# A streaming encoder layer on one core: pairs of heads and three score buffers in the second attention, single-row events, dense tiles routed earlier

## The chip, the cores and the metric

The kernel runs on one core of a Trainium2 chip. A core has a matrix engine (PE, TensorE), a vector engine (DVE, VectorE), a scalar engine (ACT, ScalarE), a general engine (POOL, GpSimd), a queue engine (SP, SyncE) and 16 DMA engines between the chip's memory and the core's own memories, SBUF and PSUM. The metric is the device time of one execution in microseconds (us), as the median of three runs.

## The reference

One layer runs over 1024 prompt frames and 32 new frames of a running stream, all in float32:

```python
proj = x @ w_in                                   # q, k, v, latents, gates
o_a = stick_breaking_attend(sb_q, k_sb, v_sb)     # first attention, 8 heads of 64
s = (q_nope @ k_nope.T + q_pe @ k_pe.T) * (64 + 32) ** -0.5
p = softmax(where(mask, s, NEG_INF))              # second attention ("MLA"), 8 heads of 64
o_b = p @ v_mla
m = (sigmoid(g_a) * (o_a @ w_oa) + sigmoid(g_b) * (o_b @ w_ob)) @ w_out
h = layer_norm(ALPHA * x + m)
# PEER: per frame and head the 16 best of 128 x 128 experts, by two lists of 128 keys
s1, i1 = top_k(q1 @ keys1.T, 16); s2, i2 = top_k(q2 @ keys2.T, 16)
top_s, pos = top_k(s1[:, None] + s2[None, :], 16)
ff = sum(softmax(top_s) * gelu(u[expert] . h) * v[expert])
y = layer_norm(ALPHA * h + ff)
```

In the second attention a frame reads all keys up to the end of its own chunk of 64 frames. The experts are 16384 pairs of rows (u, v) of 1024 elements each.

## The kernel before

Frames are cut into tiles of 128 (0 to 7) and the sample tile of 32 new frames. They are worked through in three groups, (0, 1, sample), (2, 3, 4) and (5, 6, 7), called groups 0, 1 and 2 here. Each group runs six blocks in a row: `project`, `stick_attend`, `mla_project`, `mla_attend`, `merge_norm`, `score_experts`. After the last group one more block, `dense_experts`, closes the kernel. Between two blocks stands a barrier of all engines: no engine starts the next block before every engine's own sequencer has got through its instructions of the last.

**Two ways to the experts.** For tiles 1, 2 and 3 (the dense tiles) all 16384 experts are computed as matrix products in `dense_experts`, with a table of gates in memory, `gates_by_expert`, that is zero but for the chosen experts. For the other tiles each expert row pair is gathered. One such step, a "row", is one of 16 choices of one head for 128 frames: an indirect DMA from the POOL queue (`fetch`, line 428, 1 MB into one of 9 places of a ring), a dot product on DVE (line 571), gelu and gate on ACT (528, 534), and a weighted addition on DVE four rows later (583). There are 672 rows.

**Routing** is the choice of the experts for one tile and head, a "route": 13 stages of small DVE operations (`route_stage`, `stage`, lines 640 to 670), a softmax after stage 6 and a copy of the indices after stage 12 on ACT. There are 72 routes, in the order of `self.routes`. A route of a dense tile is followed by 16 scatters: indirect DMAs of POOL that add one gate per frame into `gates_by_expert` (`scatter`, line 451). The first scatter of a head waits until all scatters of the same tile's head before have landed.

**What sets the order.** Rows and routes run as background work in the blocks of groups 1 and 2 and in the last block. `SHARES` lists for each block how many rows it takes, how many rows make one event (`batch`), how many heads are routed, and how many scatters it should take. `lay_out` spreads rows and stages evenly into one list of events per block, and `lay_out_loads` places the POOL engine's loads and scatters among them. The foreground code calls `bg.dve(part)` and `bg.act(part)` after each of its steps, which issue the events up to that share; ACT is one step behind DVE. POOL has nothing but this background work in groups 1 and 2, in the order of the events. A row's place of the ring is free when the row five steps earlier has been added.

**The second attention** (`mla_attend`) takes 24 items in each group, one per tile and head. Per item: PE computes scores into one of two score buffers (line 1287); DVE writes the mask, takes the row maximum, and scales it to the exponential's bias (1365, 1368, 1370); ACT takes the exponential with its sum (1335); PE transposes the probabilities by 128x128 (1298) into one PSUM area of 1024 columns; ACT copies them to SBUF in one operation (1346); PE multiplies them with the values, 64 columns per matmul (1309). After the eight heads of a tile DVE multiplies by the inverse sums (1380), PE transposes the result (1321) and DVE copies it to `mla_outT` (1388), which `merge_norm` reads (1506).

## Time and profile before

| | us |
|---|---|
| three runs | 3553.0, 3553.65, 3565.41 |
| median | 3553.65 |
| the profiled execution | 3558.26 |
| its span, first to last instruction | 3556.5 |

| engine | busy us | share of the span |
|---|---|---|
| PE, matmuls | 3036.3 | 85% |
| DVE | 2536.0 | 71% |
| POOL | 1558.1 | 44% |
| ACT | 1210.2 | 34% |

The blocks begin at about these times of the span (PE's first instruction in them):

| | project | stick | mla_project | mla | merge | scores |
|---|---|---|---|---|---|---|
| group 0 | 0 | 154 | 184 | 231 | 275 | 360 |
| group 1 | 436 | 643 | 777 | 827 | 948 | 1054 |
| group 2 | 1161 | 1384 | 1581 | 1638 | 1812 | 1935 |

The last block runs from 2041 to the end. The shares over the whole span are averages over blocks with different limits, so the rows further down are taken block by block. A group of instructions ends with its busy time, the mean of one, and the idle time before it with what ended it; in these, "issue" means that the profile shows nothing that the engine waited for.

### The profile page before, as it was taken

To read this page: it belongs to the slowest core of one execution; us is meant where nothing else is said; L and a number is where in the kernel's file an instruction comes from. 1 tells how busy PE (TensorE), PEld (TensorE's weight loads), DVE (VectorE), ACT (ScalarE), POOL (GpSimd) and SP (SyncE) were. 2 spreads that over 40 slices of the span, in tenths; PEclk is the share of its full clock that TensorE was granted. 3 is DMA by queue.
4 is the path that set the end of the run, shared out by engine and by line. 5 is a ranking of instruction groups with operands and counts; after the bars stand their busy time and mean duration, and the time that the engine had idled before them with its cause. 6 is when DMAs were issued, how large, how long until landed. Compare 5 with 4: busy or idle time off the path is not lost. (4 is left out here: it accounts for less than half of the span.)

```text
span 3556.5 us, 36144 instructions
## 1 busy us (share of the span) xinstructions
PE 3036.3 (85%) x10170; PEld 1717.7 (48%) x10170; DVE 2536.0 (71%) x5041; ACT 1210.2 (34%) x3181; POOL 1558.1 (44%) x1184
## 2 busy tenths in 40 slices
PE   8979989676889895775887898999989999989988
PEld 5755745344545453433654554444444444444443
DVE  0122069887786877877867678888888888788886
ACT  0241234665533435754552322222222222222221
POOL 0000025667662288888777533333333333333330
PEclk9989999785789997997688999999999999999999
DMA  4675589666799997576678999999999999999995
GB/s 144 217 254 177 190 311 394 207 181 202 222 321 359 338 341 218 145 202 181 183 248 301 406 404 399 399 405 396 404 378 412 400 407 398 397 393 407 400 408 204
DMA packets 375912, 1098.51 MB, mean 309 GB/s; under 512 B 91712, under 2 KB 210208, under 8 KB 289568
## 3 DMA queue, kind: packets, MB, share of 16 engines
q0 software_dynamic: 165072, 751.05, 56.6%
q1 hardware_dynamic: 176800, 303.85, 24.4%
q10 hardware_dynamic: 33840, 41.30, 3.3%
q8 instruction: 82, 1.34, 0.2%
q14 instruction: 118, 0.97, 0.1%
HBM read 1031.97 MB, written 63.02 MB: 308 GB/s over the span
## 5 line engine op out<-in xcount | busy, mean ns | idle before, releaser
L428 POOL DMA_INDIRECT expert_rows<-in_experts,picked_index x640 | 770.9, 1204 | 1271.1 <-DVE ff_sum L583 1157.1
L571 DVE SCALAR_TENSOR_TENSOR expert_rows<-expert_rows,h_tile 128x1024 f32<-128x1024 f32 x672 | 820.1, 1220 | 256.8 <-DMA expert_rows<-in_experts,picked_index 212.4
L583 DVE SCALAR_TENSOR_TENSOR ff_sum<-expert_rows,coefficients,ff_sum 128x1024 f32<-128x1024 f32 x672 | 860.8, 1281 | 92.2 <-ACT coefficients L534 75.9
L1786 PE MATMUL dense_act_ps<-dense_hT,key_columns 128*128 128x384 f32 x2048 | 724.7, 510 | 139.5 <-DMA key_columns<-in_key_columns 128.5
L451 POOL DMA_INDIRECT gates_by_expert<-dense_gate,gate_address x384 | 680.3, 1772 | 154.7 <-issue 129.2
L1775 PE MATMUL dense_out_ps<-dense_value_rows,dense_weights 128*128 128x512 f32 x1536 | 678.9, 592 | 0.5 <-DVE dense_weights L1854 0.5
L1786 PEld LDWEIGHTS dense_act_ps<-dense_hT,key_columns 128*128 128x128 f32 x2048 | 399.4, 198 | 482.8 <-DMA key_columns<-in_key_columns 196.2
L833 PE MATMUL proj_ps<-xT,w_in_block 128*128 128x384 f32 (+1 forms) x1392 | 424.1, 468 | 40.7 <-PEq L1595 16.5
L1775 PEld LDWEIGHTS dense_out_ps<-dense_value_rows,dense_weights 128*128 128x128 f32 x1536 | 291.8, 190 | 342.6 <-issue 309.7
L833 PEld LDWEIGHTS proj_ps<-xT,w_in_block 128*128 128x128 f32 x1392 | 268.3, 193 | 195.7 <-issue 37.9
L528 ACT ACTIVATE activated<-dots 128x1 f32<-128x1 f32 (+1 forms) x631 | 124.8, 198 | 638.5 <-DVE expert_rows L571 601.5
L1820 ACT ACTIVATE dense_weights<-dense_act_ps 128x384 f32<-128x384 f32 x128 | 62.5, 488 | 626.0 <-PE dense_act_ps L1786 614.5
L1651 PE MATMUL peer_q_ps<-hT,wq_half 128*128 128x384 f32 (+1 forms) x768 | 239.0, 471 | 16.0 <-PEq L1409 8.2
L375 ACT ACT_TABLE_LOAD x111 | 142.4, 1283 | 269.0 <-DVE top_scores L656 96.5
L1651 PEld LDWEIGHTS peer_q_ps<-hT,wq_half 128*128 128x128 f32 x768 | 148.5, 196 | 97.6 <-issue 15.1
L534 ACT ACTIVATE coefficients<-activated,expert_gate 128x1 f32<-128x1 f32 x640 | 184.1, 294 | 19.7 <-ACT activated L528 0.4
L1287 PE MATMUL score_ps<-mla_kT,mla_qT 96*128 96x512 f32 (+4 forms) x208 | 114.6, 674 | 48.6 <-PEq L1062 48.6
L404 POOL DMA_DIRECT2D expert_scores<-peer_scores x72 | 62.9, 874 | 202.3 <-POOLq L1595 202.2
L1513 PE MATMUL out_ps<-w_out,mergedT 128*128 128x512 f32 (+1 forms) x288 | 130.7, 604 | 3.4 <-DVE mergedT L1568 3.4
L1298 PE MATMUL probsT_ps<-identity,probs 128*128 128x128 f32 (+2 forms) x312 | 66.9, 360 | 67.5 <-ACT probsT L1346 51.6
L528 ACT ACT_TABLE_LOAD x88 | 112.9, 1283 | 27.1 <-DVE expert_rows L571 23.5
L1039 DVE SCALAR_TENSOR_TENSOR softplus<-log_weight_ps,abs_exp_ln 128x512 f32<-128x512 f32 (+2 forms) x78 | 50.8, 651 | 97.1 <-ACT abs_exp_ln L1015 96.5
(186 smaller groups left out, 3144.8 us busy)
## 6 DMA issues: line engine op xcount, KB each, us to landing
key_columns<-in_key_columns SPq DMA_DIRECT2D x128, 512.0 KB, 11.6
dense_value_rows<-in_experts SPq DMA_DIRECT2D x128, 512.0 KB
gates_by_expert<-zeros POOLq DMA_DIRECT2D x12, 2048.0 KB, 21.9
wq_half<-in_peer_wq SPq DMA_DIRECT2D x48, 512.0 KB
dense_gates<-gates_by_expert SPq DMA_DIRECT2D x128, 192.0 KB
w_in_block<-in_w_in ACTq DMA_DIRECT2D x18, 1024.0 KB
w_in_block<-in_w_in SPq DMA_DIRECT2D x18, 1024.0 KB
w_out<-in_w_out SPq DMA_DIRECT2D x24, 512.0 KB, 7.5
```

The source lines that it names most:

```text
L375: act.preload_act_table_set(EXP_LN)
L428: pool.indirect_dma_start(to, None, self.a["experts"], bass.IndirectOffsetOnAxis(ap=index[:, k:k + 1], axis=0)).then_inc(self.got[p % self ...
L451: pool.indirect_dma_start(self.a["gates_by_expert"], bass.IndirectOffsetOnAxis(ap=self.flat[i][:, k:k + 1], axis=0), self.dgate[i][:, k:k ...
L528: act.activation(self.gel[:, k:k + m], self.dots[:, k:k + m], ACT.Gelu).then_inc(self.gelud, m)
L534: act.activation(self.coef[:, c:c + 1], self.gel[:, c:c + 1], ACT.Identity, scale=gate[:, c:c + 1]).then_inc(self.weighed, 1)
L571: dve.scalar_tensor_tensor(place, place, 1.0, self.h[n % 2][:], ALU.mult, ALU.mult, accum_out=self.dots[:, s % TOPK:s % TOPK + 1]).then_in ...
L583: dve.scalar_tensor_tensor(total, self.ring[:, p % self.RING, D:2 * D], self.coef[:, y % TOPK:y % TOPK + 1], total, ALU.mult, ALU.add).the ...
L833: mm = nc.tensor.matmul(out[:, 0:W], w[b % 2][:, k, col:col + P], xT[:, k, :], start=(k == 0), stop=(k == KC - 1))
L1513: mm = nc.tensor.matmul(ps[2 * n + c][0:r, :], f["mergedT"][:, k, at:at + r], w_out[:, k, 512 * c:512 * (c + 1)], start=(k == 0), stop=(k ...
L1651: mm = nc.tensor.matmul(qp[2 * (h % 2) + c][:, 0:W], wq[h % 4][k // 4][:, k % 4, PKEYS * c:PKEYS * (c + 1)], f["hT"][:, k, :], start=(k == ...
L1775: mm = nc.tensor.matmul(out[d][:, 512 * half:512 * (half + 1)], w[e % AB][:, P * d:P * (d + 1)], vals[e % VB][:, 512 * half:512 * (half + ...
L1786: mm = nc.tensor.matmul(up[it % 2][:, 0:W], keys[it % KB][:, k, :], hTd[:, k, :], start=(k == 0), stop=(k == KC - 1))
```

## The change

The change touches four things.

**The second attention.** There are three score buffers of 1024 columns and the scores run two items ahead of the transposes. The transposes go into one bank of 512 columns, so an item with more than four key tiles takes two parts, each copied by ACT before the next is written; ACT's copies keep three buffers `probsT`. The product with the values is made for two heads at a time with the values as the stationary side: it gives the transposed output straight away, 64 rows for each head of the pair. ACT copies it to `mla_outT` once per tile. The scale is folded into `norm_gains` with a minus sign, so that DVE takes a minimum of negated scores and the bias needs no operation of its own. The division by the sums moves to the start of `merge_norm`: three transposes of the inverse sums, a copy on ACT, eight small matmuls that spread them over 64 rows each, and four DVE multiplications of 128x384.

**Rows.** Each row is an event of its own, and ACT collects them (`pending`) until it has `batch` of them, which is 2 in `stick` and `mla`.

**Routes of group 1's tiles.** `self.routes` takes tiles 2 and 3 in pairs two heads after tile 4's first two, so the dense tiles' heads come earlier in the list.

**Scatters.** The last column of `SHARES` for group 2 changes.

```diff
@@ SHARES @@
-        ((2, "project"), 40, 1, 9, 44), ((2, "stick"), 26, 2, 6, 72), ((2, "mla_project"), 7, 1, 2, 26), ((2, "mla"), 25, 2, 5, 70),
-        ((2, "merge"), 20, 1, 2, 48), ((2, "scores"), 29, 1, 0, 40),
+        ((2, "project"), 40, 1, 9, 62), ((2, "stick"), 26, 2, 6, 76), ((2, "mla_project"), 7, 1, 2, 26), ((2, "mla"), 25, 2, 5, 76),
+        ((2, "merge"), 20, 1, 2, 30), ((2, "scores"), 29, 1, 0, 40),
@@ lay_out @@
-        self.routes = [*ahead(0, 1), *heads(SAMPLE), *ahead(4, 2, 3), *heads(5), *heads(6), *heads(7)]
+        pairs = [[(t, h) for t in (2, 3)] for h in range(HEADS)]
+        mixed = [(4, 0), (4, 1), *pairs[0], *pairs[1], (4, 2), *pairs[2], *pairs[3], (4, 3), *pairs[4], *pairs[5], (4, 4), (4, 5), *pairs[6],
+                 (4, 6), *pairs[7], (4, 7)]
+        self.routes = [*ahead(0, 1), *heads(SAMPLE), *mixed, *heads(5), *heads(6), *heads(7)]
...
-                m = min(batch, end - row)
-                due = self.routed_before(row + m - 1) if row < end else 0
+                due = self.routed_before(row) if row < end else 0
...
-                    self.beside[block].append(("rows", row, m))
-                    row += m
+                    self.beside[block].append(("row", row))
+                    row += 1
@@ act @@
-            if e[0] == "rows":
-                self.act_rows(self.nc.scalar, range(e[1], e[1] + e[2]))
+            if e[0] == "row":
+                self.pending.append(e[1])
+                if len(self.pending) == self.batch:
+                    self.act_pending()
...
@@ mla_project @@
+            nc.vector.tensor_scalar(gain[:, 0:QC], gain[:, 0:QC], -MLA_SCALE, None, ALU.mult).then_inc(gain_scaled, 1)
@@ mla_attend, PE @@
+            scores(0)
+            scores(1)
+            for n in range(N + 1):
+                if n + 2 < N:
+                    scores(n + 2)
...
+                    for y, part in enumerate(parts(i)):
+                        if n or y:
+                            pe.wait_ge(t_copied, copies_before[n] + y)
...
+                        for par in range(2):
+                            first = HD * (h - 1 + par)
+                            mm = nc.tensor.matmul(op[half[par], P * (h // 2):P * (h // 2) + r], f["mv"][0:rows, vt, first:first + HD],
+                                                  pT[(k - 1 + par) % 3][0:rows, P * x:P * x + r], start=(x == 0), stop=(x == len(tiles) - 1),
@@ mla_attend, DVE @@
-                    nc.vector.reduce_max(mx[0:r, t:t + 1], sp[t % 2][0:r, 0:nk], AX).then_inc(max_done, 1)
-                    dve.wait_ge(max_done, t + 1)
-                    nc.vector.tensor_scalar(nm[0:r, t:t + 1], mx[0:r, t:t + 1], -MLA_SCALE, None, ALU.mult).then_inc(nm_done, 1)
+                    nc.vector.tensor_reduce(nm[0:r, t:t + 1], sp[t % 3][0:r, 0:nk], AX, ALU.min).then_inc(nm_done, 1)
...
-                    dve.wait_ge(av_done, n + 1)
...
-                    nc.vector.tensor_tensor(on[turn(i) % 2][0:r, :].rearrange("p (h d) -> p h d", h=HEADS),
...
-                    nc.vector.tensor_copy(f["obT"][:, :, g.at[i]:g.at[i] + r],
@@ merge_norm, PE @@
+                        for q in range(4):
+                            for par in range(2):
+                                pick = m["ident"][0:HEADS, 2 * q + par:2 * q + par + 1].broadcast_to([HEADS, HD])
+                                mm = nc.tensor.matmul(ps[q][HD * par:HD * par + HD, 0:W], pick, riT[0:HEADS, :], start=True, stop=True, skip_group_check=True)
+                            mm.then_inc(spread, 1)
+                        pe.wait_ge(scaled, 4)
@@ merge_norm, DVE @@
+            for q in range(4):
+                dve.wait_ge(spread, q + 1)
+                nc.vector.tensor_tensor(f["obT"][:, q, :], f["obT"][:, q, :], ps[q][:, 0:W], ALU.mult).then_inc(scaled, 1)
```

Counted in the instruction order of the two programs, POOL's scatters lie in group 2's blocks like this (group 1's counts, the rows of every block and the route stages of every block are the same in both):

| block of group 2 | project | stick | mla_project | mla | merge | scores |
|---|---|---|---|---|---|---|
| scatters before | 55 | 73 | 26 | 54 | 32 | 16 |
| scatters after | 76 | 84 | 26 | 38 | 32 | 0 |

POOL's queue in group 2's `project` where it turns from rows of the sample tile to picked rows, before; `expert_scores` is the load of a route's scores, `expert_rows` a row's fetch, `gates_by_expert` a scatter:

```order
L404 DMA expert_scores_72<-peer_scores 128x256
L451 DMA gates_by_expert<-dense_gate_142,gate_address_134 6291456x1
L428 DMA expert_rows<-in_experts,picked_index_95 128x2048
L451 DMA gates_by_expert<-dense_gate_142,gate_address_134 6291456x1 x2
L428 DMA expert_rows<-in_experts,picked_index_95 128x2048
L451 DMA gates_by_expert<-dense_gate_143,gate_address_135 6291456x1 x2
L428 DMA expert_rows<-in_experts,picked_index_95 128x2048
```

The same place after:

```order
L417 DMA expert_scores_72<-peer_scores 128x256
L464 DMA gates_by_expert<-dense_gate_143,gate_address_135 6291456x1
L441 DMA expert_rows<-in_experts,picked_index_95 128x2048
L464 DMA gates_by_expert<-dense_gate_143,gate_address_135 6291456x1 x2
L441 DMA expert_rows<-in_experts,picked_index_95 128x2048
L464 DMA gates_by_expert<-dense_gate_143,gate_address_135 6291456x1 x3
L441 DMA expert_rows<-in_experts,picked_index_95 128x2048
L464 DMA gates_by_expert<-dense_gate_143,gate_address_135 6291456x1 x2
L464 DMA gates_by_expert<-dense_gate_144,gate_address_136 6291456x1
```

Between two fetches stand two to three scatters where one or two stood.

PE's queue for two heads of tile 5 in group 2's `mla_attend`, before, with its waits (a semaphore keeps the name of the block that used its number first):

```order
L1287 MATMUL score_ps<-mla_kT_244,mla_qT_246 128x512 [waits sp_done]
L1287 MATMUL score_ps<-mla_kT_244,mla_qT_246 128x256
L1298 MATMUL probsT_ps<-identity,probs_14153 128x128 [waits rest_done,sp_done]
L1298 MATMUL probsT_ps<-identity,probs_14153 128x128 x5
L1309 MATMUL mla_out_ps<-mla_v_245,probsT_14154 128x64 [waits rest_done]
L1309 MATMUL mla_out_ps<-mla_v_245,probsT_14154 128x64 x5
L1287 MATMUL score_ps<-mla_kT_244,mla_qT_246 128x512 [waits sp_done]
L1287 MATMUL score_ps<-mla_kT_244,mla_qT_246 128x256
```

And after, where `mla_ps_turned_0` takes the transposes and `mla_ps_turned_1` the output:

```order
L1300 MATMUL score_ps<-mla_kT_246,mla_qT_248 128x512 [waits ln_done]
L1300 MATMUL score_ps<-mla_kT_246,mla_qT_248 128x256
L1317 MATMUL mla_ps_turned_0<-identity,probs_14093 128x128 [waits sp_masked,ln_done]
L1317 MATMUL mla_ps_turned_0<-identity,probs_14093 128x128 x3
L1317 MATMUL mla_ps_turned_0<-identity,probs_14093 128x128 [waits sp_masked]
L1317 MATMUL mla_ps_turned_0<-identity,probs_14093 128x128
L1329 MATMUL mla_ps_turned_1<-probsT_14097,mla_v_247 64x128 [waits sp_masked]
L1329 MATMUL mla_ps_turned_1<-probsT_14095,mla_v_247 64x128
```

The transposes of one item are now in two parts with a wait between them, and the product with the values stands only behind every second item.

## Rows read from the trace of the kernel before

**Rows 1.** Windows: us, busy per engine (count), TensorE clock, DMA share, GB/s.

```profile
core 0: us, PE busy (x) PEld busy (x) DVE busy (x) ACT busy (x) POOL busy (x), PEclk, DMA share, GB/s
230.70:274.60 43.90, 35.15 (x205) 24.63 (x205) 18.84 (x73) 19.45 (x90) 4.37 (x6) 0.80 0.89 342
274.60:359.60 85.00, 79.60 (x249) 43.16 (x249) 25.89 (x45) 11.96 (x22) 0.00 (x0) 0.96 0.56 180
642.70:777.00 134.30, 95.14 (x526) 54.15 (x526) 113.74 (x264) 93.36 (x186) 88.21 (x62) 0.80 0.56 166
826.70:947.50 120.80, 94.94 (x364) 69.79 (x364) 99.19 (x259) 69.57 (x164) 89.25 (x61) 0.60 0.61 182
...
1638.10:1812.10 174.00, 135.15 (x613) 103.74 (x613) 132.80 (x311) 95.45 (x174) 132.26 (x89) 0.73 0.57 161
1812.10:1935.00 122.90, 95.03 (x248) 49.33 (x249) 88.98 (x167) 44.61 (x90) 94.61 (x61) 0.87 0.94 316
1935.00:2041.50 106.50, 95.84 (x352) 60.57 (x352) 69.30 (x88) 28.54 (x98) 65.41 (x46) 0.95 1.05 397
2041.50:3501.00 1459.50, 1330.12 (x3475) 670.53 (x3476) 1205.52 (x2084) 350.67 (x1160) 505.47 (x431) 0.97 0.99 398
```

**Rows 2.** Groups of POOL's instructions from 1246.2 to 1770.9.

```profile
L451 POOL DMA_INDIRECT gates_by_expert<-dense_gate,gate_address x192 | 338.7, 1764 | 62.2 <-issue 61.3 <-DVE ff_sum L583 0.6 <-POOLq L1062 0.3
L428 POOL DMA_INDIRECT expert_rows<-in_experts,picked_index x66 | 73.9, 1119 | 20.1 <-issue 19.8 <-POOLq L686 0.3
...
L428 POOL DMA_INDIRECT expert_rows<-in_experts,sample_index x14 | 16.8, 1198 | 4.3 <-issue 4.3
```

**Rows 3.** Timeline around the end of group 2's `mla_project`: start, us, instruction.

```profile
1626.66 0.20 ACT L484 CAST picked_index<-expert_f 128x16 uint32<-128x16 f32 x1 [0.48 <-DVE picked L669]
...
1636.23 1.58 POOL L451 DMA_INDIRECT gates_by_expert<-dense_gate,gate_address  x1 [0.30 <-issue]
1638.03 0.37 SPq L1263 DMA_DIRECT2D w_o<-in_w_oa  x1
...
1638.11 1.55 POOL L451 DMA_INDIRECT gates_by_expert<-dense_gate,gate_address  x1 [0.30 <-POOLq L1062]
...
1641.05 0.11 DVE L1365 MEMSET score_ps<- 64x64 f32 x1 [14.43 <-PE score_ps L1287]
```

**Rows 4.** Group of POOL's scatters from 1626.7 to 1641, where DVE stands still.

```profile
L451 POOL DMA_INDIRECT gates_by_expert<-dense_gate,gate_address x7 | 11.0, 1566 | 2.1 <-issue 1.8 <-POOLq L1062 0.3
```

**Rows 5.** Groups of DVE and ACT in group 2's `mla`, 1638.1 to 1812.1.

```profile
L571 DVE SCALAR_TENSOR_TENSOR expert_rows<-expert_rows,h_tile 128x1024 f32<-128x1024 f32 x25 | 30.4, 1217 | 10.1 <-DMA expert_rows<-in_experts,picked_index 10.1
L1370 DVE TENSOR_SCALAR minus_max<-row_max 128x1 f32<-128x1 f32 x24 | 3.7, 153 | 0.8
L1380 DVE TENSOR_TENSOR mla_out<-mla_out_ps,inverse_sum 128x512 f32<-128x512 f32 x3 | 2.1, 692 | 0.1
L1388 DVE COPY mla_outT<-mla_outT_ps 128x512 f32<-128x512 f32 x3 | 2.1, 684 | 0.8 <-PE mla_outT_ps L1321 0.8
L1346 ACT COPY probsT<-probsT_ps 128x768 f32<-128x768 f32 (+2 forms) x24 | 21.5, 896 | 1.0 <-PE probsT_ps L1298 1.0
```

**Rows 6.** Waits in the same stretch: engine, for what, us, times, longest.

```profile
DVE score_ps L1365 <- PE score_ps L1287: 24.5, 5, 14.4
DVE inverse_sum L1378 <- PE mla_out_ps L1309: 10.5, 3, 7.6
```

**Rows 7.** Timeline of PE at full clock: one item's parts, and the first attention's product.

```profile
1733.53 0.93 PE L1298 MATMUL probsT_ps<-identity,probs 128*128 128x128 f32 x7
1734.29 1.67 PE L1309 MATMUL mla_out_ps<-mla_v,probsT 128*128 128x64 f32 x14
...
710.11 1.09 PE L954 MATMUL stick_out_ps<-weights,sb_v 128*64 128x128 f32 x16
```

**Rows 8.** Waits in group 1's `mla`, 826.7 to 947.5.

```profile
DVE score_ps L1365 <- PE score_ps L1287: 20.8, 3, 16.7
DVE inverse_sum L1378 <- PE mla_out_ps L1309: 5.4, 1, 5.4
DVE mla_outT L1388 <- PE mla_outT_ps L1321: 4.9, 3, 2.5
```

**Rows 9.** Instructions of a DVE multiplication of 128x384 with one side in PSUM.

```profile
L1220 DVE TENSOR_TENSOR rope_q<-mla_ps,cosT x2: 537/548/558, 1586.4 to 1599.0; 128x384 f32<-128x384 f32 x2
```

**Rows 10.** Waits of DVE for rows in group 2's `project`, 1246 to 1384.

```profile
DVE expert_rows L571 <- DMA expert_rows<-in_experts,sample_index: 15.4, 7, 3.9
...
DVE expert_rows L571 <- DMA expert_rows<-in_experts,picked_index: 4.7, 4, 1.4
```

190 lines of the change are left out of this document (93 added, 97 removed).

## The prediction

> **What bounds the kernel now.** I read the profile in three steps: the windows block by block, then the groups and waits of one engine in the stretches where the change acts, then the timeline at a block's end. The windows [rows 1] show three kinds of block. The last block and the `scores` blocks move 397 to 398 GB/s at a DMA share of 0.99 to 1.05: they are bound by transfers, and the last block's 1459.5 us carry the same 400 fetches in both programs, so nothing in it moves. The two attentions have a DMA share of 0.56 to 0.61, and in group 1 and 2 DVE is the busiest engine, 99.2 of 120.8 us and 132.8 of 174.0 us in `mla`. Group 0's `mla` has no background work; there PE is busy 35.2 of 43.9 us.
>
> The third kind is seen only on POOL. From 1246.2 to 1770.9, which is 524.7 us from group 2's first scatter to late in its `mla`, POOL runs 192 scatters, 80 fetches and a few plain loads, and all its idle time is put down to "issue", about 0.3 us ahead of each [rows 2]. Busy and idle of these groups add to 338.7+62.2+73.9+20.1+16.8+4.3 = 516 us of the 524.7. So POOL is full for four blocks, though a share of 44% over the whole span hides it. That this binds the others is seen at one place: at the end of `mla_project` ACT does its last work at 1626.66 (DVE as well, within 0.3 us), POOL goes on with scatters, and at 1638.03 the next block opens, when POOL's own sequencer passes its branch; DVE's idle time there is 14.4 us [rows 3]. Counting the program's order against the trace, 12 fetches and scatters of the block were still queued on POOL at that moment, 10 at the end of `project`, 11 at the end of `stick`. I read this as a queue that is full at all three ends: a block ends when POOL has about a dozen left.
>
> **The price of a scatter** in the full stretch is (338.7+62.2)/192 = 2.09 us with its gap [rows 2]. Where DVE stands still it is 1.57+0.30 = 1.87 us [rows 4]. Between these two ends I take 1.87, since scatters are added where the other engines would wait for POOL.
>
> The Trainium skill (SBUF — State Buffer, Who interferes with whom) says that a VectorE operation with two SBUF inputs and a GpSimd instruction that reads SBUF exclude each other, and that the one that comes later "fully blocks". The direction agrees with the rows: 1764 ns on average beside DVE work and 1566 without it [rows 2, 4]. The size doesn't: full blocking by operations of 1.22 us (571) would add 0.6 us on average, not 0.2. By the page each added scatter would cost 2.5 us instead of 1.9, which is the fourth case below.
>
> **Part 1: scatters moved forward.** Up to the end of group 2's `mla_project` the order has 76+84+26 = 186 scatters where it had 55+73+26 = 154, with the same fetches, and the first scatter stands at the same place of the queue. POOL was never idle there, so 32 x 1.87 = **+60 us** until group 2's `mla` opens (67 by the other price). It can't be hidden: POOL is the last engine. The lower bound is +55, if the queue takes one or two more at the ends. In return POOL has 38 instead of 54 scatters in `mla` and none instead of 16 in `scores`. The latter is bound by transfers, and a scatter's own transfers are small; 29 fetches at 1 MB stay. For `scores` and for `merge`, which starts with less queued on POOL, I take **-7 us** (0 to -12).
>
> **Part 2: the second attention in group 2.** DVE loses 3.7 us of bias operations, 2.1 of multiplications and 2.1 of copies [rows 5], so 132.8 becomes 125. Of the 41 us in which it was idle, 10.5 were waits for the product with the values [rows 6], gone because the division is made later; 24.5 were waits for scores, of which 14.4 began before the block and 10 should mostly go with the third buffer; 10.1 were waits for gathered rows [rows 5], which shrink as POOL gets 16 scatters fewer. With 125 of work, 3 at the start, 7 of small gaps and some 10 of waits left, DVE alone gives 145. PE gains too: seven key tiles' product took 1.67 us, 239 ns each, at full clock; the first attention's products of the new form, 64 rows and 128 columns, take 1.09 us for eight, 136 ns [rows 7]. That is 168 x 0.10 = 17 us of PE work less. Against it stands the copy in two parts: a second wait of PE for ACT and of ACT for PE per item. Four transposes take 0.93 x 4/7 = 0.53 us at full clock and double at half, and with two handovers that is 1 to 1.3 us of ACT's time for each of 24 items, 24 to 31 us beside 95.5 us busy: 120 to 127, below DVE's 145 but near. PE's clock was 0.73 here [rows 1], between its two levels; at the lower one its work of 5 us or more per item comes near DVE's as well. I take 150 instead of 174: **-24 us** (-10 to -38).
>
> POOL allows this: a dozen queued operations (22 us) plus 38 x 2.09 + 25 x 1.42 = 115 us, 137 us in all.
>
> **Part 3: group 1 and group 0.** In group 1 only tile 4 needs two parts. DVE's 99.2 us lose 7.9, of 21.6 idle us 5.4 + 4.9 wait for products and transposes that are gone, and 4 of the score waits lie inside [rows 8]: **-13 us** (-5 to -20). Group 0 has 24 items in 43.9 us with PE at 35.2; half of the product with the values goes: **-8 us** (-4 to -11). Single rows let a foreground operation wait for one row, 2.5 us on DVE, not two. That can matter in group 1's `stick`, where DVE is busy 113.7 of 134.3 us and POOL isn't full: **-4 us** (-10 to +2). In group 2 it is hidden behind POOL.
>
> **Part 4: the merge.** PE now waits at the first step for transposes, a copy, eight small matmuls and four DVE multiplications of 0.55 us [rows 9]. The matmuls run beside the multiplications, so about 4 us per group. In group 0 nothing hides it (PE 79.6 of 85.0 [rows 1]): +4; in groups 1 and 2 transfers hide part: +2 and +1. Against that the attention's tail, multiplication, transposes and copy, is shorter, which part 2 and 3 contain. Sum **+7 us** (0 to +12). The scaling of the gains is one tiny operation per group behind a load that arrives before its first use: 0, and 0.5 us if uncovered.
>
> **The sum**, on the profiled span: 60 - 7 - 24 - 13 - 8 - 4 + 7 = +11 us. The profiled execution took 3558.3, so 3569; it was 4.6 us above the median of the runs, so against 3553.65 the forecast is **3565 us**, with a range of its own of 3540 to 3582.
>
> **The rivals.**
> Forecast, 3565: POOL's queue is the bound of group 2 up to `mla`, and what the attention wins is given back there. Chance 0.57.
> POOL keeps pace with others rather than setting it. For it speaks that DVE waited only 15.4+4.7 = 20 us for gathered rows in that part of `project` [rows 10]. Against it speaks the end of `mla_project` [rows 3]. Then the 60 us vanish: 3505. Chance 0.10.
> ScalarE becomes the bound of the second attention (the other side). The place is the one bank for transposes; it decides from the point where ACT's time for an item, 4.0 us busy plus the handover, exceeds DVE's 5.2 to 6, so if the handover costs over 2 us. Then group 2 wins nothing and group 1 only 5: 3565 + 24 + 8 = 3597. For it speaks that ACT is strictly in order with table loads between. Chance 0.25.
> The full block of the page named above: 32 x 0.6 = 20 us on top of the forecast, 3584. Rows 2 and 4 speak against. Chance 0.08.
>
> **How the numbers follow.** 0.5% of 3553.65 is 17.8 us, about what a measurement of this kernel can tell from no change: the bounds are 3536 and 3571. Faster than that: nearly all of the second case and a little of the forecast, 0.10. Slower: most of the third and fourth and the upper end of the forecast, 0.37. Between: 0.53. For 8 in 10 the range reaches from 3536 to 3598; the second case is left out.
>
> **What would show it.** On POOL no idle time beyond 0.3 us from group 2's first scatter to its `mla`, and `mla` of group 2 opening about 60 us later, less what group 0 and 1 gave; `project` longer by some 40 us and `stick` by some 20. In group 2's `mla` about 150 us, the line of waits of DVE for scores near 10 us, ACT waiting for PE between two copies of an item for about a microsecond. If `project` of group 2 is no longer than before, part 1 is wrong. If the second attention doesn't shrink in group 1, where POOL is not full, parts 2 and 3 are.

## The result, and the profile after

The changed kernel takes **3609.84 us** (median of four runs, 3606.52 to 3618.47), the kernel before 3553.32. The ratio is 1.0159, with a 95% interval of 1.0139 to 1.0178: the change makes the kernel slower by 56 us. The forecast was 3565 with a range up to 3598: the direction came out, the size didn't, and the measured time lies 12 us above the range. The profiled execution of after took 3608.89 us with a span of 3607.1, so 50.6 us more span than before.

In the changed kernel a fetch is at line 441, a scatter at 464, DVE's two operations of a row at 584 and 596. In the second attention the scores are at 1300, the transposes at 1317, the product at 1329, the exponential at 1345, the copy of the transposes at 1356, the minimum at 1384.

The blocks of before that the rows ahead of the prediction don't have, windows over group 2's `project`, `stick` and `mla_project` (columns as in rows 1; `stick` is cut here, and in the table below, at ACT's first activation, 2 us behind its opening, every other block where it opens; the time 1161 given for the start of group 2's `project` ahead of the prediction should be 1173):

```profile
1172.80:1386.20 213.40, 182.84 (x548) 103.50 (x550) 168.22 (x408) 75.42 (x200) 135.98 (x102) 0.92 0.93 311
1386.20:1574.90 188.70, 137.87 (x860) 78.01 (x858) 162.14 (x354) 138.57 (x275) 159.16 (x104) 0.89 0.57 161
1574.90:1638.10 63.20, 31.94 (x111) 15.56 (x111) 40.78 (x100) 28.96 (x63) 53.16 (x35) 0.79 0.83 223
```

The same windows of after: `mla` and `merge` of group 0; `stick`, `mla` and `merge` of group 1; all six blocks of group 2.

```profile
core 0: us, PE busy (x) PEld busy (x) DVE busy (x) ACT busy (x) POOL busy (x), PEclk, DMA share, GB/s
228.10:268.70 40.60, 33.71 (x193) 20.40 (x194) 11.60 (x43) 21.51 (x92) 4.36 (x6) 0.63 0.97 371
268.70:358.10 89.40, 83.46 (x267) 44.73 (x268) 27.70 (x49) 12.35 (x23) 0.00 (x0) 0.94 0.53 172
641.70:772.60 130.90, 86.36 (x500) 49.61 (x498) 112.69 (x263) 86.84 (x176) 89.78 (x61) 0.83 0.55 155
...
826.80:937.90 111.10, 74.89 (x352) 45.56 (x353) 90.40 (x229) 72.97 (x174) 91.06 (x61) 0.70 0.67 190
937.90:1048.60 110.70, 96.10 (x268) 49.72 (x268) 84.03 (x162) 45.37 (x96) 69.98 (x45) 0.89 0.95 315
...
1167.50:1418.80 251.30, 182.65 (x548) 103.51 (x550) 168.28 (x408) 75.43 (x200) 169.30 (x122) 0.85 0.85 272
1418.80:1627.00 208.20, 144.36 (x860) 79.01 (x857) 162.63 (x354) 138.83 (x275) 175.09 (x115) 0.84 0.53 136
1627.00:1691.10 64.10, 33.82 (x110) 16.46 (x110) 40.78 (x101) 28.96 (x63) 54.07 (x35) 0.77 0.83 229
1691.10:1863.90 172.80, 109.97 (x600) 72.30 (x600) 124.78 (x281) 98.54 (x198) 115.50 (x80) 0.79 0.59 176
1863.90:1979.20 115.30, 96.02 (x268) 49.62 (x268) 90.70 (x172) 45.50 (x91) 82.79 (x52) 0.90 0.96 315
1979.20:2093.90 114.70, 97.57 (x352) 61.28 (x352) 68.79 (x87) 28.54 (x98) 34.88 (x30) 0.92 0.98 372
```

`project` of group 2 is 38 us longer and `stick` 19.5, with the same busy time of PE, DVE and ACT to within a few us (PE in `stick` 144 for 138) and only POOL busier, 169.3 for 136.0 and 175.1 for 159.2. `mla` of group 2 has 25 us less work on PE and 8 less on DVE than in rows 1, and is 172.8 us long where it was 174.0. Those two facts are the result: a loss that was forecast, and a gain that didn't come.

At the end of group 2's `project` the timeline of after shows what rows 3 showed elsewhere (start, us, instruction, idle time before it):

```profile
1407.38 0.31 ACT L495 ACTIVATE gate_address<-expert_f,dense_token 128x16 uint32<-128x16 f32 x1 [1.61 <-DVE expert_f L683]
...
1414.77 1.58 POOL L464 DMA_INDIRECT gates_by_expert<-dense_gate,gate_address  x1 [0.30 <-issue]
1416.58 1.28 ACT L388 ACT_TABLE_LOAD   x1 [8.89 <-PEq L699]
...
1416.65 1.55 POOL L464 DMA_INDIRECT gates_by_expert<-dense_gate,gate_address  x1 [0.30 <-POOLq L699]
```

DVE and ACT stand still for 9 us while POOL scatters; at the same place of before, ACT stood still for 1.8 us (1382.24 to 1384.02). POOL's groups from 1240.9 to 1739 answer rows 2: no idle time but the gap of 0.3 us.

```profile
L464 POOL DMA_INDIRECT gates_by_expert<-dense_gate,gate_address x191 | 329.0, 1723 | 58.1 <-issue 56.9 <-DVE ff_sum L596 0.3 <-POOLq L908 0.3
L441 POOL DMA_INDIRECT expert_rows<-in_experts,picked_index x53 | 62.3, 1175 | 16.1 <-issue 16.1
```

Waits in group 2's `mla` of after, which answer rows 6 (engine, for what, us, times, longest):

```profile
PE mla_ps_turned L1317 <- ACT probsT L1356: 60.4, 25, 6.2
...
ACT probsT L1356 <- PE mla_ps_turned L1317: 35.5, 31, 3.7
...
DVE expert_rows L584 <- DMA expert_rows<-in_experts,picked_index: 25.2, 10, 4.8
...
DVE score_ps L1381 <- PE score_ps L1300: 14.9, 2, 13.8
```

The waits of DVE for scores inside the block are gone, as forecast (13.8 of the 14.9 lie at its start). What has grown are the waits of PE for ACT and of ACT for PE, on the same 48 small steps. Before, ACT waited 1.0 us for transposes (last line of rows 5) and PE 26.8 us for the copies:

```profile
L1298 PE MATMUL probsT_ps<-identity,probs 128*128 128x128 f32 x168 | 33.5, 362 | 36.7 <-ACT probsT L1346 26.8 <-ACT probs L1335 10.0
```

And DVE waits 25.2 us for rows, where it was 10.1.

### The profile page after: what moved, and what is told of

The parts are those of the page before. It is cut to its first block and busy times, and to the rows that moved or that the text cites. A ratio compares the mean times of both kernels' runs of the same rounds, so it can differ in the third digit from the quotient of the medians.

```text
span 3607.1 us, 36135 instructions
## 1 busy us (share of the span) xinstructions
PE 3000.2 (83%) x10191; PEld 1659.9 (46%) x10191; DVE 2517.1 (70%) x4966; ACT 1221.4 (34%) x3223; POOL 1542.1 (43%) x1184
## 5 line engine op out<-in xcount | busy, mean ns | idle before, releaser
L1807 PE MATMUL dense_act_ps<-dense_hT,key_columns 128*128 128x384 f32 x2048 | 719.5, 507 | 142.2 <-DMA key_columns<-in_key_columns 131.1
L464 POOL DMA_INDIRECT gates_by_expert<-dense_gate,gate_address x384 | 671.7, 1749 | 154.3 <-issue 118.9
L547 ACT ACTIVATE coefficients<-activated,expert_gate 128x1 f32<-128x1 f32 x640 | 184.0, 294 | 19.4
L1317 PE MATMUL mla_ps_turned<-identity,probs 128*128 128x128 f32 (+2 forms) x312 | 66.9, 334 | 97.2 <-ACT probsT L1356 94.8
L1300 PE MATMUL score_ps<-mla_kT,mla_qT 96*128 96x512 f32 (+4 forms) x208 | 107.4, 640 | 46.8 <-PEq L1075 46.8
L541 ACT ACT_TABLE_LOAD x87 | 111.6, 1283 | 28.7 <-DVE expert_rows L584 25.1
```

The lines of the kernel that those rows point to most:

```text
L464: pool.indirect_dma_start(self.a["gates_by_expert"], bass.IndirectOffsetOnAxis(ap=self.flat[i][:, k:k + 1], axis=0), self.dgate[i][:, k:k ...
L541: act.activation(self.gel[:, k:k + m], self.dots[:, k:k + m], ACT.Gelu).then_inc(self.gelud, m)
L547: act.activation(self.coef[:, c:c + 1], self.gel[:, c:c + 1], ACT.Identity, scale=gate[:, c:c + 1]).then_inc(self.weighed, 1)
L1807: mm = nc.tensor.matmul(up[it % 2][:, 0:W], keys[it % KB][:, k, :], hTd[:, k, :], start=(k == 0), stop=(k == KC - 1))
```

## Experiments

All lengths of blocks below come from one profiled execution of each kernel, all ratios from comparison with the kernel before in the same series. The kernel before had medians of 3557.6, 3553.0 and 3554.3 us in the three series, so a difference between medians of two series is good to some 5 us only. This table is worked out from the traces: the length of a block in us and, in brackets, its scatters.

| run | median us | project 2 | stick 2 | mla_project 2 | mla 2 | merge 2 + scores 2 | stick 1 | mla 1 |
|---|---|---|---|---|---|---|---|---|
| before | 3553.3 | 213.4 (55) | 188.8 (73) | 63.1 (26) | 174.0 (54) | 229.3 (48) | 125.8 | 120.9 |
| changed | 3609.8 | 251.2 (76) | 208.2 (84) | 64.1 (26) | 172.8 (38) | 230.0 (32) | 131.0 | 111.1 |
| scatters_back | 3535.9 | 216.1 (55) | 187.6 (74) | 64.0 (26) | 167.2 (54) | 219.7 (47) | 131.6 | 111.5 |
| attention_only | 3551.3 | 217.1 (55) | 189.4 (73) | 61.3 (26) | 170.8 (54) | 232.0 (48) | 126.1 | 109.0 |
| background_only | 3618.4 | 252.4 (76) | 210.5 (84) | 63.2 (26) | 177.7 (38) | 224.9 (32) | 132.0 | 117.5 |
| few_scatters_new | 3513.2 | 200.9 (20) | 182.9 (20) | 52.5 (8) | 167.7 (8) | 223.0 (8) | 131.4 | 111.5 |
| few_scatters_old | 3508.1 | 200.8 (16) | 189.1 (16) | 52.6 (8) | 163.6 (12) | 217.4 (12) | 125.8 | 121.5 |
| few_whole_items | 3487.1 | 201.2 (20) | 184.1 (20) | 53.3 (8) | 142.2 (8) | 221.4 (8) | 130.9 | 108.0 |
| few_copy_first | 3492.5 | 200.9 (20) | 182.6 (20) | 52.0 (8) | 143.2 (8) | 221.0 (8) | 131.0 | 111.6 |
| early_spread | 3536.6 | 215.4 (68) | 185.2 (65) | 55.5 (18) | 167.3 (49) | 231.4 (56) | 131.5 | 111.5 |
| changed_whole_items | 3604.2 | 253.5 (76) | 207.2 (84) | 64.3 (26) | 165.0 (38) | 234.3 (32) | 131.5 | 107.1 |
| back_whole_items | 3529.8 | 214.4 (55) | 187.3 (74) | 64.1 (26) | 154.2 (54) | 229.1 (47) | 131.5 | 106.9 |
| early_whole_items | 3514.9 | 205.6 (59) | 184.8 (67) | 55.9 (16) | 143.3 (46) | 246.7 (68) | 131.5 | 107.0 |
| early_whole_pairs | 3521.1 | 207.1 (59) | 186.0 (67) | 57.4 (16) | 142.0 (46) | 242.8 (68) | 128.1 | 107.4 |

### Which part costs: three runs that undo or do one alone

**Scatters put back**, all else as changed:

```diff
-        ((2, "project"), 40, 1, 9, 62), ((2, "stick"), 26, 2, 6, 76), ((2, "mla_project"), 7, 1, 2, 26), ((2, "mla"), 25, 2, 5, 76),
-        ((2, "merge"), 20, 1, 2, 30), ((2, "scores"), 29, 1, 0, 40),
+        ((2, "project"), 40, 1, 9, 44), ((2, "stick"), 26, 2, 6, 64), ((2, "mla_project"), 7, 1, 2, 26), ((2, "mla"), 25, 2, 5, 54),
+        ((2, "merge"), 20, 1, 2, 32), ((2, "scores"), 29, 1, 0, 18),
```

> The changed kernel with other numbers in the scatter column of SHARES, so that group 2's blocks have 55, 74, 26, 54, 32, 15 scatters (before 55, 73, 26, 54, 32, 16; changed 76, 84, 26, 38, 32, 0). Routes, single rows and second attention stay as changed. Theory A (POOL's queue binds group 2 from its first scatter to its mla, and the scatters moved forward are what the change lost): project falls from 251 to about 213 us, stick from 208 to about 189, scores from 115 to about 107, mla stays between 165 and 176; in all 3610 - 57 - 8 = 3545 us, 3535 to 3556. Theory B (the single-row events or the order of the routes lengthened project and stick): both blocks stay near 251 and 208 and the time stays above 3590.

Measured: 3535.86 us, ratio to before 0.9942 (0.9921 to 0.9962), 74 us less than changed. `project` and `stick` fall by 35 and 21 us, `mla` by 6, `merge` and `scores` together by 10. Theory A holds, at the lower end of its range. The 10 us of `merge` and `scores` are not shown to come from the scatters: with the same scatter counts the two took 219.7 us here and 229.1 in `back_whole_items`. Windows of this run over group 2's `project`, `stick` and `mla`:

```profile
1164.80:1380.90 216.10, 182.12 (x548) 103.17 (x550) 168.30 (x408) 75.46 (x199) 139.88 (x102) 0.92 0.91 309
1380.90:1568.50 187.60, 139.22 (x860) 77.38 (x858) 161.92 (x354) 138.68 (x275) 157.86 (x104) 0.90 0.60 159
...
1632.50:1799.70 167.20, 110.29 (x600) 72.06 (x600) 125.04 (x281) 98.16 (x198) 140.62 (x93) 0.79 0.65 177
```

Up to `mla` the three blocks have 31 scatters fewer than changed and are together 55.8 us shorter, 1.80 us a scatter, with nothing else altered. Five numbers of one table are thus the whole loss: with them put back the rest of the change is a gain.

**The attention alone**, the kernel before with the hunks of `mla_project`, `mla_attend` and `merge_norm`:

> The kernel before with the new second attention and its merge alone; events, routes and scatters as before. Theory A (POOL binds group 2): the attention is worth about 10 us in group 1's mla and 3 in group 0's, merge gives back 4 each in groups 0 and 1, and group 2's mla stays at 170 to 174 since its rows still come behind the scatters; 3553 - 13 + 8 - 2 = 3546 us, 3538 to 3553. Theory C (the transposes in two parts bind the new attention): group 2's mla stays at 172 or more as well, group 1's at 111; the same total. A gain of 20 us or more in group 2's mla would say that the attention is faster there and that the scatters or events took it away.

Measured: 3551.33 us, ratio 0.9982 (0.9969 to 0.9995). Group 1's `mla` gives 12 us, group 2's only 3. The total is 5 us above the expectation and in its range. (The profiled execution was the fastest of ten, 3541.9, so the block lengths of this row are on the short side.)

**The background alone**, the kernel before with the hunks of `SHARES`, `lay_out` and `act`:

> The kernel before with the changed background alone: single-row events, ACT taking two, dense tiles' routes earlier, scatters 76, 84, 26, 38, 32, 0 in group 2's blocks. The second attention and the merge are the old ones. Theory A: project and stick are 38 and 20 us longer than before, scores 8 longer, mla of group 2 with 38 instead of 54 scatters 0 to 10 us shorter: 3553 + 57 + 8 - 5 + 5 (group 1's stick) = 3618 us, 3605 to 3630. Theory B' (the new attention is what costs): 3553 to 3570.

Measured: 3618.38 us, ratio 1.0162 (1.014 to 1.0184), as theory A said to 1 us. `project` is 39 us longer and `stick` 22, with the old attention. That the total agrees so closely is luck: `mla` of group 2 has 16 scatters fewer and is 4 us longer, not shorter, while `merge` and `scores` are together 4 us shorter where `scores` alone was to be 8 longer. Neither is explained here.

### Why the second attention gives nothing in group 2: four runs with POOL out of the way

**Few scatters, new kernel.** Each head of tiles 2 and 3 has 4 scatters instead of 16 (the waits that count them go by 4 as well):

```diff
-                waiting += [(e[1], c) for c in range(TOPK)]
+                waiting += [(e[1], c) for c in range(n_gates(self.routes[e[1]][0]))]
...
+PKEYS, TOPK, EXPERTS = 128, 16, 128 * 128; n_gates = lambda t: TOPK if t == 1 else 4
```

> The changed kernel with 4 instead of 16 scatters for each head of tiles 2 and 3: 64 instead of 256 scatters in group 2. It leaves 12 of 16 gates of these tiles out of the table, so their results lack those experts. Theory A: with POOL no longer full, project falls to about 200 us (it was 251), stick to about 175 (208), mla_project to about 52 (64), and mla of group 2, where rows came late behind scatters, to about 150 (173); in all 3610 - 51 - 33 - 12 - 23 = 3491 us, 3475 to 3510. Theory C (ACT's and PE's handover of transposes in two parts binds group 2's mla, whatever POOL does): mla stays at 168 us or more, total about 3512.

Measured: 3513.23 us, ratio 0.9871 (0.9852 to 0.9891). `project` and `mla_project` fall to the lengths that theory A gave (200.9, 52.5), `stick` only to 182.9. But `mla` stays at 167.7: theory C, and so does the total, 3513 for its 3512. Group 2's `mla` in this run, window and waits, PE's and ACT's for each other and DVE's:

```profile
1601.70:1769.40 167.70, 109.13 (x600) 71.25 (x600) 124.35 (x281) 98.29 (x198) 42.80 (x38) 0.80 0.53 180
```

```profile
PE mla_ps_turned L1317 <- ACT probsT L1356: 55.9, 25, 5.1
ACT probsT L1356 <- PE mla_ps_turned L1317: 39.8, 31, 4.9
DVE ff_sum L596 <- ACT coefficients L547: 14.0, 7, 6.6
DVE score_ps L1381 <- PE score_ps L1300: 13.9, 6, 3.6
```

POOL has 43 us of work in 168, and no engine is busier than 124. PE and ACT wait for each other 96 us in all, and DVE 28 us for what the two owe it, ACT's coefficients of the rows and PE's scores. So the waits for scores inside the block are back here.

**Few scatters, old kernel**, the same edit:

> The kernel before with 4 instead of 16 scatters for each head of tiles 2 and 3 (64 instead of 256 in group 2; 12 of 16 gates of these tiles are left out of the table). It shows the old second attention in group 2 with POOL out of the way; the new one took 167.7 us there. Theory A' (the new attention is faster only by the DVE work that it drops, some 6 to 10 us, and POOL hid that): old mla of group 2 takes 172 to 178 us here as well. Theory D (the old attention gains as much as the new one once POOL is free, the form of the attention is worth nothing in group 2): 165 to 169 us. Project, stick and mla_project as in the run with few scatters of the new kernel: 201, 178 to 183, 52.

Measured, in a single execution: 3508.11 us, and `mla` of group 2 takes 163.6, shorter than theory D had it and 8 us under theory A'. The old attention is 4 us faster than the new one there, with 23 us more PE work and 8 more DVE work. So the new form loses in group 2 all that it saves; whether it loses 4 us more, one execution of each can't tell.

**Whole items.** Two score buffers instead of three, two banks for the transposes, one copy an item:

```diff
-        sp = [s.enter_context(nc.psum_tensor(f"score_ps{3 * g.n + i}", [P, 1024], F32)) for i in range(3)]
-        tp, op = banks(nc, s, f"mla_ps_turned{g.n}_", 2)
+        sp = [s.enter_context(nc.psum_tensor(f"score_ps{2 * g.n + i}", [P, 1024], F32)) for i in range(2)]
+        tp = s.enter_context(nc.psum_tensor(f"mla_probsT_ps{g.n}", [P, 1024], F32)); op, = banks(nc, s, f"mla_ps_turned{g.n}_", 1)
...
-        parts = lambda i: [keys_of(i)[2][c:c + 4] for c in range(0, len(keys_of(i)[2]), 4)]
+        parts = lambda i: [keys_of(i)[2]]
```

> The changed kernel with few scatters (64 in group 2, 12 of 16 gates left out) and, in the second attention, two score buffers instead of three and two banks for the transposes, so that an item is transposed and copied in one part; the scores run one item ahead. All else as in the run with few scatters of the new kernel (3513 us, mla of group 2 167.7, of group 1 111.5). Theory C (the handover of two parts between PE and ACT binds group 2's mla: PE waited 56 us there for ACT's copies): mla of group 2 falls to 150 to 158 us, group 1's by 2 to 4; total 3493 to 3503. Theory E (what binds is the order DVE minimum, exponential, copy within an item, and the third buffer matters more than the parts): mla stays at 166 to 175, total 3510 to 3522.

Measured: 3487.13 us, ratio 0.9808 (0.978 to 0.9837), 26 us under `few_scatters_new` (22 by the two ratios). `mla` of group 2 falls by 25.5 us, more than theory C had said, group 1's by 3.5. Group 0's, where every item has one part in both kernels, grows from 40.4 to 46.0; there the third buffer is worth something.

**The copy first.** Three buffers and two parts, but ACT copies an item's first part before the next item's exponential instead of behind it:

```diff
                 if t < N:
...
+                    if t >= 1:
+                        copy(t - 1, 0)
                     act.wait_ge(nm_done, t + 1)
-                    if t >= 2:
-                        act.wait_ge(t_done, copies_before[t - 1])
                     bg.exp_ln(act)
...
-                    for y, part in enumerate(parts(i)):
-                        act.wait_ge(t_done, copies_before[n] + y + 1)
+                    for y in range(1 if t < N else 0, len(parts(items[n][0]))):
+                        copy(n, y)
```

> The changed kernel with few scatters (12 of 16 gates of tiles 2 and 3 left out) and one change of order on ACT in the second attention: the first part of an item's transposes is copied before the next item's exponential, the second part after it. PE then holds no second part behind an exponential that waits for DVE. Theory C: mla of group 2 falls from 167.7 to 155 to 160 us, total about 3503. Theory E (the exponential comes later and DVE's next step with it): mla stays within 3 us of 167.7 or grows.

Measured: 3492.52 us, ratio 0.9815 (0.9783 to 0.9848). `mla` of group 2 falls to 143.2 us, more than theory C had said: the place of the copy in ACT's order is worth 24 us, and two parts with three buffers come within 1 us of one part with two. Group 1's stays at 111.6, so the 3.5 us that whole items gave there are not the order's, and their cause is open. (Group 0 loses 6.5 us by it; ACT waits there 23 us for transposes, 12 in the changed kernel.) Windows over group 2's `mla`, of the whole items and of the copy first:

```profile
1602.70:1744.90 142.20, 99.92 (x600) 66.59 (x601) 123.75 (x281) 94.39 (x174) 44.60 (x38) 0.83 0.61 211
```

```profile
1609.50:1752.70 143.20, 104.47 (x600) 66.78 (x600) 124.01 (x281) 96.52 (x198) 44.68 (x38) 0.82 0.61 210
```

DVE is now busy 124 of 142 us and sets the pace. Its waits with the copy first, where the lines above had 14.0 and 13.9 us:

```profile
DVE score_ps L1384 <- PE score_ps L1300: 3.6, 1, 3.6
DVE ff_sum L596 <- ACT coefficients L547: 2.8, 3, 1.8
```

These two lines hold 21.5 of the 24.5 us gained. PE and ACT still wait for each other 66 us (36.3 and 29.6) in this run: such waits cost only where they reach DVE. How the two parts held DVE up is seen in one item near the end of the run with few scatters of the new kernel (PE, DVE and ACT):

```profile
1739.72 1.28 ACT L541 ACT_TABLE_LOAD   x1
1740.64 0.60 PE L1317 MATMUL mla_ps_turned<-identity,probs 128*128 128x128 f32 x4
...
1741.76 1.28 ACT L388 ACT_TABLE_LOAD   x1
...
1743.05 1.11 ACT L1345 ACTIVATE probs<-score_ps,minus_max 128x1024 f32<-128x1024 f32 x1
...
1744.15 0.58 ACT L1356 COPY probsT<-mla_ps_turned 128x512 f32<-128x512 f32 x1
...
1744.79 0.66 PE L1317 MATMUL mla_ps_turned<-identity,probs 128*128 128x128 f32 x4 [3.54 <-ACT probsT L1356]
...
1745.37 3.14 PE L1329 MATMUL mla_ps_turned<-probsT,mla_v 128*64 128x128 f32 x32
...
1745.48 0.59 ACT L1356 COPY probsT<-mla_ps_turned 128x512 f32<-128x512 f32 x1 [0.75 <-PE mla_ps_turned L1317]
...
1746.07 1.12 ACT L1345 ACTIVATE probs<-score_ps,minus_max 128x1024 f32<-128x1024 f32 x1
...
1748.44 2.44 PE L1300 MATMUL score_ps<-mla_kT,mla_qT 96*128 96x512 f32 x4
...
1750.72 0.60 PE L1317 MATMUL mla_ps_turned<-identity,probs 128*128 128x128 f32 x4
...
1750.96 0.11 DVE L1381 MEMSET score_ps<- 64x64 f32 x1 [2.61 <-PE score_ps L1300]
...
1751.41 0.59 ACT L1356 COPY probsT<-mla_ps_turned 128x512 f32<-128x512 f32 x1 [4.14 <-PE mla_ps_turned L1317]
```

PE has made the first part by 1741.24 and stands at the second (3.54 us), because the copy of the first lies in ACT's queue behind the gelu of two rows with its two table loads and behind the next item's exponential. ACT works without a pause from 1739.72 on; it doesn't wait for DVE here, though over the block it waited 23.5 us for DVE's minima before exponentials. Once freed, PE has a product of 3.14 us and scores of 2.44 to do before the next transposes, and now ACT stands (4.14), and DVE with it (2.61). In this item the long work of one engine doesn't lie beside that of the other. The last copy of the run with whole items, at the same place:

```profile
1739.22 1.01 ACT L1355 COPY probsT<-mla_probsT_ps 128x1024 f32<-128x1024 f32 x1 [0.74 <-PE mla_probsT_ps L1316]
```

It waits 0.74 us for PE, since all transposes of the item stand ahead of the product in PE's queue.

### Two causes on one block, and what POOL allows

**Changed kernel with whole items** in groups 1 and 2 (`SB = 2 if g.n else 3`, parts of 8 tiles instead of 4 where `g.n` isn't 0), scatters as changed:

> The changed kernel with all its scatters (76, 84, 26, 38, 32, 0) and one edit: in groups 1 and 2 the second attention has two score buffers and two banks for transposes, one part per item; group 0 keeps three buffers. With few scatters this edit took 25 us from group 2's mla and 3 from group 1's. Theory A (POOL binds the blocks before it, not this one, once 38 scatters are left in it): mla of group 2 falls from 173 to about 148 us, which is what the prediction had taken for the change; total 3610 - 24 - 3 = 3583 us, 3573 to 3592. Rival (the rows that come late behind the dozen queued scatters keep the block long): mla 160 or more, total 3597 or more.

Measured: 3604.2 us, ratio 1.0139 (1.0109 to 1.0169). `mla` of group 2 is 165.0 us: the rival's side. With its window, waits and groups this block reads:

```profile
1682.10:1847.10 165.00, 110.18 (x600) 74.19 (x600) 124.70 (x281) 94.35 (x174) 113.70 (x80) 0.75 0.61 179
```

```profile
DVE expert_rows L584 <- DMA expert_rows<-in_experts,picked_index: 22.2, 9, 4.7
...
1736.00:1763.00 27.00, 17.23 (x96) 12.30 (x96) 23.24 (x53) 18.48 (x36) 6.08 (x5) 0.75 0.51 179
```

So group 2's `mla` has two causes, and to take either one away gives little: 172.8 as changed, 167.7 with few scatters, 165.0 with whole items, 142.2 with both. DVE's waits for rows, 22.2 us here and none in `few_whole_items`, make nearly the whole difference of the last two (22.8). POOL's work in the block is less than its length (113.7 us busy and 80 gaps of 0.3, 138 us), but it isn't spread. POOL is full for the first 40 us, then it waits 15.9 us for places of the ring (it runs 5 operations in the 27 us of the last line), and from about 80 us on it is full again. The rival's time came, but not by its reason: only 5.0 of the 22.2 us lie in the first 40, behind the queued dozen, and 17.4 in the second full stretch, from 98 us on.

**Scatters put back, with whole items:**

> The run with the scatters put back (55, 74, 26, 54, 32, 15; 3536 us) with the same edit of the second attention in groups 1 and 2. Theory A: POOL has 54 scatters, 25 rows and 12 queued operations in group 2's mla, 171 us of work in a block of 167, so POOL takes over as its bound: mla falls by 5 to 12 us only, group 1's by 3; total about 3525 us, 3517 to 3532. Rival (POOL doesn't bind this block): mla about 143, total 3508 to 3513.

Measured: 3529.8 us, ratio 0.9928 (0.99 to 0.9956). `mla` falls by 13 us, to 154.2, and ends with 11 operations queued on POOL where it had 3. POOL is busy 130.1 us with 85 gaps of 0.3, 156 us in all, so it is the block's bound, theory A, though it gave a little more than was said. The block is also 11 us shorter than in the run above with 16 scatters more in it: here they are spread (5 to 9 in every 20 us), POOL never waits for a place, and rows are late by 16.4 us instead of 22.2. `merge` and `scores` take back 9 of the 13, so the total gains 6.

**Early routes, scatters spread**, two score buffers not yet in it:

```diff
-        mixed = [(4, 0), (4, 1), *pairs[0], *pairs[1], (4, 2), *pairs[2], *pairs[3], (4, 3), *pairs[4], *pairs[5], (4, 4), (4, 5), *pairs[6],
+        mixed = [*pairs[0], (4, 0), *pairs[1], (4, 1), *pairs[2], (4, 2), *pairs[3], (4, 3), *pairs[4], *pairs[5], (4, 4), (4, 5), *pairs[6],
```

> The changed kernel with two other tables: the routes of group 1's tiles begin with head 0 of tiles 2 and 3 instead of two heads of tile 4, so that group 2's first scatter can run some 45 us earlier, and the scatters are spread 68, 65, 18, 49, 32, 24 over group 2's blocks. Theory A (POOL's queue is the bound wherever it is full, and was idle for the first 75 us of group 2): no block is POOL-bound any more, project 201 to 206 us, stick 183 to 186, mla_project 52 to 58, mla 165 to 168, as with few scatters; total 3513 to 3525 us, 10 to 23 below the run with the scatters put back (3536). Rival (scatters cost by their transfers and their port, not by POOL's queue): no better than 3536.

Measured: 3536.56 us, ratio 0.9947 (0.9922 to 0.9972): missed by nearly 12 us. The total is the rival's; the blocks speak for theory A, since `stick` and `mla_project`, with fewer scatters, came down to its lengths. `stick`, `mla_project` and `mla` came out as expected, but `project`, with 68 scatters, is 215.4 and not 201 to 206, with 198 us of it filled by POOL's work and gaps and 11 operations queued when the next block opened, and `merge` and `scores` take 231 us with 56 scatters. I had put too much into `project`; the time came from one block and went to others.

**Early routes, fewer scatters in `project` and `mla`, whole items:**

> The same attention with the early routes, scatters 59, 67, 16, 46, 36, 32 over group 2's blocks. Theory A: POOL's work is now near each block's length without it: project about 204, stick 185, mla_project 54, mla 145 to 150, merge and scores together 228 us; total about 3505 us, 3495 to 3515. Rival (whatever is taken from one block POOL gives to the next, its 256 scatters and 147 fetches fill group 2 as a whole): 3520 to 3530.

Measured: 3514.86 us, ratio 0.9881 (0.9853 to 0.9908), the best kernel with all its work, 39 us under before and 95 under changed. Windows over group 2:

```profile
1164.10:1369.70 205.60, 183.87 (x548) 103.79 (x550) 167.33 (x408) 76.15 (x200) 156.21 (x107) 0.94 0.96 325
...
1610.40:1753.70 143.30, 101.50 (x600) 67.18 (x600) 123.66 (x281) 94.37 (x174) 120.76 (x80) 0.81 0.71 206
1753.70:1874.20 120.50, 94.48 (x268) 48.84 (x268) 90.89 (x171) 45.37 (x91) 90.59 (x56) 0.90 0.94 306
1874.20:2000.40 126.20, 96.47 (x352) 60.84 (x352) 70.00 (x87) 28.62 (x98) 98.33 (x64) 0.88 0.99 329
```

The blocks up to `mla` are as theory A said; `merge` and `scores` are 19 us longer than it said, since 68 scatters and 49 rows fill POOL for 224 of their 247 us. The total lies at the upper end of theory A's range and below the rival's. But the rival is half right: over group 2 POOL's work and gaps fill 793 of 836 us. With 64 scatters instead of 256 the same attention took 3487 us (`few_whole_items`), so some 28 us are left to be had from fewer or cheaper scatters; whether another spread gives any of it was not tried.

**The same with rows two and two** in the blocks whose `batch` is 2:

```diff
-                due = self.routed_before(row) if row < end else 0
+                m = min(batch, end - row)
+                due = self.routed_before(row + m - 1) if row < end else 0
...
-                    self.beside[block].append(("row", row))
-                    row += 1
+                    self.beside[block] += [("row", s) for s in range(row, row + m)]
+                    row += m
```

> As the run before it (early routes, whole items, scatters 59, 67, 16, 46, 36, 32), but the rows of stick, mla_project and mla are laid out two and two, one behind the other, as in the kernel before. It tests what lengthened group 1's stick from 126 to 131 us in every run with the changed background. Theory F (single rows, for which ACT waits until it has two): stick of group 1 falls by 4 to 6 us, group 2's stays or gains up to 6. Rival (the order of the routes): stick stays at 131. Total equal or 5 to 10 us less than the run before.

Measured: 3521.12 us, ratio 0.9904 (0.9872 to 0.9937). Group 1's `stick` is 128.1 us, so 3.4 of the 5 to 6 us that single rows and the new routes cost there come back; a bit less than theory F had, and the rest stays open. The total doesn't gain.

## Why the prediction was wrong, step by step

Against the span of before, block by block (us):

| step | forecast | measured |
|---|---|---|
| part 1, POOL up to `mla` | +60 | +58.2 (37.8, 19.4 and 1.0) |
| `merge` and `scores` of group 2 | -7, and +1 of part 4 | +0.7 |
| part 2, `mla` of group 2 | -24 | -1.2 |
| part 3, `mla` of groups 1, 0 | -13, -8 | -9.8, -3.4 |
| part 3, `stick` of group 1 | -4 | +5.2 |
| part 4, `merge` of groups 0, 1 | +4, +2 | +4.4, +4.4 |
| all other blocks (`mla_project` of group 0 alone -3.8) | 0 | -7.9 |
| sum | +11 | +50.6 |

**Part 1 was right**, in mechanism and size. The 32 scatters cost 58.2/32 = 1.82 us each, beside the 1.87 taken from rows 4. `scatters_back` (2.4 us over before in these blocks) and `background_only` show that little else made them longer, and the runs with few scatters show how far POOL had bound the kernel before already: 13 us of `project` and 10 of `mla_project`. The second rival (3505) falls. So does the fourth, with its 2.5 us a scatter: the trace has 1.82 a scatter at the block's length and 1723 ns plus 0.3 on POOL. By the Trainium skill (SBUF — State Buffer, Who interferes with whom) a VectorE operation with two SBUF inputs contends with a GpSimd instruction that reads SBUF, under an exclusive lock. No run here isolates the port or shows whether a scatter is such an instruction, so what falls is the price, not the rule.

**Part 2 is the step that failed**, 22.8 of the 39.6 us by which the span was missed: -24 was forecast for group 2's `mla` and -1.2 measured. Its sentence was that the copy in two parts costs ACT 24 to 31 us, "120 to 127, below DVE's 145". The size was near: ACT waited 35.5 us there. The error was to compare sums of engines as if they ran beside each other. The two handovers put PE's and ACT's work of an item one behind the other, and the order of ACT's queue (row work, exponential of the next item, then the copy that PE waits for) passed the delay on to DVE, as late scores and late coefficients. The working never wrote down the order of one item over the three engines. `few_whole_items` and `few_copy_first` show it: DVE is busy 124 us in both as in `few_scatters_new`, ACT 94 and 97 for 98, and the block is 25 us shorter. The third rival had the right place, the one bank for transposes, and a time (3597) 13 us below the measured one, but its reason wasn't the mechanism. It asked for over 2 us of handover an item and had ACT as the bound; 35.5/24 is 1.5 us, and ACT itself waited 29 us inside the block for DVE's minima (23.8+19.9 less the 14.7 at its opening).

A second error lies in the sentence "POOL allows this", 137 us of POOL work. It too was a sum against a length; the scatters came in two full stretches with a pause between, and rows were late by 25.2 us. `changed_whole_items` shows that this alone would have kept the block at 165. With either cause the forecast of 150 fails.

**Part 3** had the sign right in both `mla` blocks and was too large by 3 and 5 us; in group 1 `few_whole_items` gives 3.5 us more, `few_copy_first` none. In group 0 I had counted PE's work as the bound; the trace of after has PE busy 33.7 us, only 1.4 less than in rows 1, at a granted clock of 0.63 where it was 0.80. Its **`stick`** term had the wrong sign. It was read from a window that reaches 6.4 us into the next block: DVE was busy 113.2 of the block's own 125.8 us (644.8 to 770.6), so there was less to win than the 134.3 suggested. A finer grain of rows was to shorten a wait; in the trace ACT collects two rows before it works on them, and DVE's waits in the block grow: for ACT from 5.5 to 9.2 us, for PE from 3.4 to 6.1. `attention_only` (126.1) puts it on the background, and `early_whole_pairs` (128.1 for 131.5) puts 3.4 us of it on the rows.

**Part 4** was right for group 0. In groups 1 and 2 the lengths of `merge` and `scores` are no measure of it: with the same code, rows and scatters in group 1, `merge` and `scores` together took between 220.2 (`changed_whole_items`) and 229.6 us (changed) in the kernels with the new merge. The 7 us expected from fewer scatters in group 2 lie inside that scatter as well.

## What to carry to other kernels

What a handover between two engines costs is set by what stands around it in both queues (24 us here between two places of one copy): before an item is cut into parts, write down for one item who stands at the head of each in-order queue, and ask what long work lies behind it. An engine that is full over a stretch of blocks pays for every operation moved into the stretch, whatever its share of the whole span is, and work that fits a block by its sum can still come too late where it is bunched: ask for the sum of each stretch, not of the block. When a block has two bounds, each alone is worth little, so one undone cause that brings nothing proves nothing about it.

## What the runs showed of the hardware

When the next block opened, POOL had 11 or 12 fetches and scatters of group 2's `project` not yet started, 9 to 12 of `stick` and 12 of `mla_project`, in all kernels that have 55 or more, 73 or more and 26 scatters in these blocks (counted in the program's order against the trace; the prediction's 10 for `project` was counted 2 us later), and none in the runs with few scatters. In the kernel before, `mla` opened at 1638.0 and the last of the 12 started at 1660.9. POOL's sequencer was thus over 20 us ahead of its work, and a barrier of sequencers doesn't say that the engine is done.

Clearing POOL shortened `stick` of group 2 by only 4.7 us with the new background (187.6 to 182.9) and not at all with the old one (188.8 and 189.1), though POOL was full there from end to end: a full queue isn't a bound by itself, yet 10 scatters more than it had (84 for 74) cost 20.6 us.
